# A two-layer attention and expert kernel: softmax work by slices of two duos, and one head's scaling moved to VectorE

## The reference

```python
h = rmsnorm(x, ln_mix[i])
qkv = h @ w_qkv[i]
q = rmsnorm(qkv[..., :nq].reshape(B, S, N_HEADS, HEAD_DIM), q_norm[i])
k = rmsnorm(qkv[..., nq:nq + nk].reshape(B, S, N_KV_HEADS, HEAD_DIM), k_norm[i])
v = qkv[..., nq + nk:].reshape(B, S, N_KV_HEADS, HEAD_DIM)
if i % N_MIXERS == 0:
    q = apply_axial_rope(q, row_cs, col_cs)
    k = apply_axial_rope(k, row_cs, col_cs)
    o = global_attention(q, k, v)          # softmax(q k^T * SCALE) v
else:
    o = window_attention(q, k, v, rel_bias, sinks[i // N_MIXERS])   # with a bias, a window and a sink
x = x + o @ w_o[i]
x = x + hier_moe(rmsnorm(x, ln_ffn[i]), w_group[i], w_expert[i], w1[i], w3[i], w2[i])
```

## Time and profile before

| | us |
|---|---|
| median of 3 runs | 674.86 |
| lowest and highest | 673.85, 676.22 |
| the profiled execution, its own time | 675.01 |
| its span, first to last instruction | 673.2 |
| TensorE busy | 639.0 |
| VectorE, ScalarE, GpSimd busy | 202.7, 177.0, 71.1 |

### The profile page before, as it was taken

One profiled execution on the slowest core, in us unless ns is written; L12 is line 12 of the kernel. 1 busy time (PEld: TensorE's weight loads), 2 busy tenths in 40 slices (PEclk: granted clock), 3 DMA queues, 4 the chain that ended last, 5 costly groups with the idle time before them and its releaser, 6 DMA issues.

```text
span 673.2 us, 7941 instructions
## 1 busy us (share of the span) xinstructions
PE 639.0 (95%) x2947; PEld 283.6 (42%) x2947; DVE 202.7 (30%) x614; ACT 177.0 (26%) x425; POOL 71.1 (11%) x85
## 2 busy tenths in 40 slices
PE   8999899899999999999999887998999999999996
PEld 5444445633433433432354444455344344334332
DVE  1655433512302302301243655234113113113112
ACT  2126642302212112112131554321212112112112
POOL 0006550000000000000010576200000000000000
PEclk9999999899999999999999999997999999999998
DMA  8999706579997999999999993484999799999993
GB/s 323 277 295 422 274 1 272 227 312 421 422 423 294 424 421 423 421 422 421 403 295 249 411 406 79 147 364 153 423 421 422 318 401 421 422 423 423 422 423 125
DMA packets 42882, 229.61 MB, mean 341 GB/s; under 512 B 8207, under 2 KB 8497, under 8 KB 18274
## 3 DMA queue, kind: packets, MB, share of 16 engines
q1 hardware_dynamic: 41212, 224.66, 85.0%
q0 software_dynamic: 1312, 4.23, 2.0%
q10 hardware_dynamic: 326, 0.31, 0.2%
HBM read 228.10 MB, written 1.08 MB: 340 GB/s over the span
## 4 chain that ended last, share of the span: by engine, by line
PE 79%; DMA 9%; DVE 5%; POOL 2%; ACT 2%; issue 1%; SPq 0%; DVEq 0%; POOLq 0%; ACTq 0%
PE ps L1304 28%; PE ps L1331 15%; PE ps L1086 11%; DMA attw<-in_w_dram 8%; PE ps L1168 6%; PE ps L1271 5%; PE ps L1283 4%; POOL attw L413 2%; PE ps L1121 2%; PE ps L1150 2%; PE ps L1137 1%; PE ps L1235 1%; DVE attw L799 1%; PE ps L1313 1%; DMA ring<-in_ln_mix_dram 1%
## 5 line engine op out<-in xcount | busy, mean ns | idle before, releaser
L1304 PE MATMUL ps<-attw,work 128*64 128x512 f32 x512 | 111.7, 592 | 1.5 <-DMA attw<-in_w_dram 1.5
L1304 PE MATMUL ps<-ring,work 128*64 128x512 f32 x512 | 111.4, 593 | 0.0
L1086 PE MATMUL ps<-attw,work 128*128 128x512 f32 x192 | 88.2, 603 | 0.3 <-DVE work L695 0.3
L1331 PE MATMUL ps<-ring,work 128*64 128x512 f32 x384 | 85.7, 595 | 1.1
L931 DVE COPY work<-ps 32x512 f32<-32x512 f32 x64 | 43.7, 683 | 106.1 <-PE ps L1331 105.7
L923 DVE TENSOR_TENSOR work<-work,ps 128x512 f32<-128x512 f32 x16 | 11.0, 688 | 190.3 <-PE ps L1304 190.3
L1304 PEld LDWEIGHTS ps<-attw,work 128*64 128x64 f32 x512 | 36.7, 137 | 75.1 <-issue 71.6
L1304 PEld LDWEIGHTS ps<-ring,work 128*64 128x64 f32 x512 | 36.5, 137 | 72.4 <-issue 72.3
L601 ACT COPY work<-ps 32x512 f32<-32x512 f32 x64 | 36.9, 576 | 107.3 <-PE ps L1331 106.9
L413 POOL TENSOR_SCALAR attw<-attw,stat 128x256 f32<-128x256 f32 x64 | 58.8, 932 | 50.2 <-DVE stat L814 50.0
L1168 PE MATMUL ps<-attw,work 128*128 128x512 f32 x128 | 59.7, 601 | 0.7 <-issue 0.5
(11 more groups left out here) (149 smaller groups left out, 486.4 us busy)
## 6 DMA issues: line engine op xcount, KB each, us to landing
ring<-in_w_dram SPq DMA_DIRECT2D x112, 1024.0 KB, 17.9
attw<-in_w_dram SPq DMA_DIRECT2D x80, 1024.0 KB, 17.5
attw<-in_w_qkv_dram SPq DMA_DIRECT2D x4, 2048.0 KB, 21.0
attw<-in_w_o_dram SPq DMA_DIRECT2D x8, 1024.0 KB, 22.6
attw<-in_w_qkv_dram SPq DMA_DIRECT2D x4, 1024.0 KB, 15.5
ring<-bias_rows POOLq DMA_DIRECT2D x16, 256.0 KB, 6.9
x_sb<-in_x_dram SPq DMA_DIRECT2D x2, 512.0 KB, 6.3
out_dram<-x_sb SPq DMA_DIRECT2D x2, 512.0 KB, 3.6
```

The lines of the kernel that those rows point to most:

```text
L1086: last = pe.matmul(ps[:, g, :], xT[:, k, P * tt:P * tt + P], wqkv[part][:, k, :], start=(k == 0), stop=(k == KB - 1))
L1304: last = pe.matmul(ps[64 * e:64 * e + 64, 6 + which, :], xg[:, k, c:c + 2 * SLOTS], w13(which, k // 4)[:, e, k % 4, :], start=(k == 0), st ...
L1331: last = pe.matmul(ps[64 * e:64 * e + 64, half, :], hT[:, k, 64 * e:64 * e + 64], w2(kh)[:, e, k % 2, 512 * half:512 * half + 512], start= ...
```

## The change

1. `scale_probs` on GpSimd scales head 0 of a duo only. VectorE scales head 1 in `invert_sum`, directly behind the reciprocal (it waits for its own reciprocal's count), and counts a new semaphore `p1_ready`. `turn_probs` turns head 1's two blocks first, behind `p1_ready`, and then waits for `p_ready` and turns head 0's.
2. VectorE's loop goes by slices: both maxima of a slice, then both inversions. The pieces of `head_norm(4)` stand: 0 and 1 at the end of slice 1, 2 between the maxima and the inversions of slice 2, 3 at the end of slice 2; those of `head_norm(5)` the same in slices 3 and 4. `copy_o` stands between the two inversions of slices 3, 5 and 7.
3. `turn_q(2)` and `turn_q(3)` stand ahead of the turning of duo 5 and duo 9; ScalarE's `copy_q(2)` and `copy_q(3)` between `exps` and `copy_probs` of u = 7 and 11; and `square_heads` with `inverse_head_rms` of groups 4 and 5 together behind `copy_probs(1)` and `copy_probs(5)`.

```diff
@@ scale_probs, GpSimd
                 pool.wait_ge(rc_ready, DUOS * L + u + 1)
-                for h in range(2):
-                    last = pool.tensor_scalar(prob[:, u % 4, h, :], prob[:, u % 4, h, :], rc[:, u % 4, h:h + 1], None, ALU.mult)
-                last.then_inc(p_ready, 1)
+                pool.tensor_scalar(prob[:, u % 4, 0, :], prob[:, u % 4, 0, :], rc[:, u % 4, 0:1], None, ALU.mult).then_inc(p_ready, 1)
@@ ScalarE's loop
                 exps(1)
-                square_heads(4)
                 exps(2)
                 copy_probs(0)
                 for u in range(3, DUOS):
                     exps(u)
-                    if u == 3:
-                        inverse_head_rms(4)
-                    if u == 7:
-                        square_heads(5)
-                    if u == 9:
-                        inverse_head_rms(5)
+                    if u in (7, 11):
+                        copy_q((u + 1) // 4)
                     copy_probs(u - 2)
-                    if u == 5:
-                        copy_q(2)
-                    if u == 11:
-                        copy_q(3)
+                    if u in (3, 7):
+                        square_heads(3 + (u + 1) // 4)
+                        inverse_head_rms(3 + (u + 1) // 4)
@@ invert_sum, VectorE
                 dve.reciprocal(rc[:, u % 4, :], total).then_inc(rc_ready, 1)
+                dve.wait_ge(rc_ready, DUOS * L + u + 1)
+                dve.tensor_scalar(prob[:, u % 4, 1, :], prob[:, u % 4, 1, :], rc[:, u % 4, 1:2], None, ALU.mult).then_inc(p1_ready, 1)
@@ VectorE's loop
-                duo_max(L, 0)
-                for u in range(1, DUOS):
-                    duo_max(L, u)
-                    invert_sum(L, u - 1)
-                    if 2 <= u < 6:
-                        head_norm(L, 4, u - 2)
-                    if 8 <= u < 12:
-                        head_norm(L, 5, u - 8)
-                    if u % 4 == 3 and u >= 7:
-                        copy_o(L, u // 4 - 1)
-                invert_sum(L, DUOS - 1)
+                for v in range(SLICES):
+                    g = 4 + v // 3
+                    duo_max(L, 2 * v)
+                    duo_max(L, 2 * v + 1)
+                    if v in (2, 4):
+                        head_norm(L, g, 2)
+                    invert_sum(L, 2 * v)
+                    if v % 2 == 1 and v >= 3:
+                        copy_o(L, v // 2 - 1)
+                    invert_sum(L, 2 * v + 1)
+                    if v in (1, 3):
+                        head_norm(L, g, 0)
+                        head_norm(L, g, 1)
+                    if v in (2, 4):
+                        head_norm(L, g, 3)
@@ turn_probs, TensorE
-                    pe.wait_ge(p_ready, DUOS * L + u + 1)
+                    pe.wait_ge(p1_ready, DUOS * L + u + 1)
...
-                    for t in range(TT):
-                        for h in range(2):
+                    for h in (1, 0):
+                        if h == 0:
+                            pe.wait_ge(p_ready, DUOS * L + u + 1)
+                        for t in range(TT):
@@ TensorE's loop
+                    if v in (2, 4):
+                        turn_q(1 + v // 2)
                     turn_probs(2 * v + 1)
-                    if v == 1:
-                        turn_q(2)
-                    if v == 4:
-                        turn_q(3)
```

More of the change, by code:

```diff
@@ L211, in encoder @@
         qkn_ready, turned, turn_copied = sem("qkn_ready"), sem("turned"), sem("turn_copied")
-        scored, max_ready, exp_done, rc_ready, p_ready = sem("scored"), sem("max_ready"), sem("exp_done"), sem("rc_ready"), sem("p_ready")
+        scored, max_ready, exp_done, rc_ready = sem("scored"), sem("max_ready"), sem("exp_done"), sem("rc_ready")
+        p_ready, p1_ready = sem("p_ready"), sem("p1_ready")
         pt_done, pt_copied, pv_done, o_copied = sem("pt_done"), sem("pt_copied"), sem("pv_done"), sem("o_copied")
```

## The result

| | before | changed |
|---|---|---|
| median, us | 674.36 (4 runs) | 685.36 (4 runs) |
| lowest and highest | 673.75, 676.22 | 683.11, 685.95 |
| ratio, 95% interval | | 1.0165 (1.014 to 1.0191) |
| the profiled execution, its span | 675.01, 673.2 | 685.91, 683.9 |
| TensorE, VectorE, GpSimd busy | 639.0, 202.7, 71.1 | 642.0, 215.0, 46.5 |

The account below looks back on a forecast made before the run. TensorE was taken as the bound, so only its pauses count. 675.0 + 4.2 (layer 0) + 1.0 (layer 1) + 2.4 (clock) = 682.6, less 0.15 for the median: 682.5 us; range 677.0 to 688.5.

Parts of the forecast that it names:

- Direction and mechanism: Attention: turnings 3 and 7 wait through ScalarE's copy and exponentials for maxima behind norm pieces; slower, chance 0.83.
- Turning 3 of layer 0: Turning of duo 3's probabilities: 6.3 us behind turning 1, starting at 63.5 instead of 61.82, +1.7 us.
- Turning 7: Layer 0, turning of duo 7's probabilities: 6.2 us behind the first output copy instead of 3.5, +2.7 us.
- The sum of the two stages: Attention without the clock: +4.2 us in layer 0 and +1.0 us in layer 1.
- The clock: TensorE's clock falls behind two of the four new attention pauses, 1.2 us each: +2.4 us.
- rival 2: TensorE's clock falls behind all four new pauses, at up to 1.8 us each: 687.4 us; chance 0.07.
- VectorE's scaling: VectorE's new 128x256 scaling behind the reciprocal takes 0.25 us, between bounds of 0.17 and 0.47.
- Rival 3: VectorE blocked by GpSimd's scaling for a whole 0.92 us each time: +8 us, 688.5 us; chance 0.08.
- Rival 4: Attention: head_norm's pieces no obstacle, only waits for GpSimd count; 7.2 us go, 667.8 us; chance 0.08.
- Passing the shift on one to one: Any shift of attention's end reaches the kernel's end in full, as expert loads start at points TensorE's progress releases.

Follow-up runs that it names:

- a3: Changed kernel with piece 1 of the norms of query groups 4 and 5 moved behind the next slice's two maxima: 675.78 us.
- b2: Changed kernel with ScalarE's copy of turned probabilities ahead of the next exponentials and two query copies one duo earlier; VectorE's order kept: 669.28 us.
- b1_awake_short: Changed kernel with 10 unused filling matmuls on TensorE ahead of turnings 3 and 7 of both layers: 684.21 us.
- c1_after_again: The changed kernel itself, unedited, timed again: 685.19 us.
- a2: Changed kernel with the split scaling taken back, so GpSimd scales both heads and the new order stays: 684.48 us.
- a1: Kernel before with the split scaling alone, VectorE scaling head 1 and GpSimd head 0, old order kept: 674.33 us.
- b3_split_copy_first: Kernel before with the split scaling and ScalarE's copy of turned probabilities ahead of the next exponentials: 668.87 us.
- b4: Changed kernel's split scaling kept, VectorE's and ScalarE's orders rearranged: most copies ahead of exponentials two duos on, norm pieces spread between maxima: 662.60 us.
- c3: Kernel before with only ScalarE's copy of turned probabilities put ahead of the next exponentials; GpSimd scales both heads: 676.15 us.
- a4: Changed kernel with 20 unused filling matmuls on TensorE ahead of turnings 3 and 7 of both layers: 685.37 us.
- c2: Changed kernel with 10 filling matmuls ahead of turnings 3 and 7 of both layers, timed again: 684.50 us.

## Why the prediction was right, point by point

**Direction and mechanism: right.** The pauses were laid out at 3.2 and 3.7 us in layer 0 and 3.6 and 4.3 in layer 1, and measured 2.90, 3.43, 3.26 and 3.98, each 0.3 shorter. Turning 3 of layer 0 was to start 6.3 us behind the end of turning 1 and starts 6.27 behind it. Turning 7 was to start 6.2 us behind the first output copy and starts 6.17 behind it, at 77.69. The copy in VectorE's timeline:

```profile
71.52 0.69 DVE L816 COPY work<-ps 128x512 f32<-128x512 f32 x1 [5.05 <-PE ps L1151]
```

a3 and b2 cut the path at two of its links and the pauses go.

**The sum of the two stages: right.** Laid out +4.2 and +1.0 us without the clock. b1_awake_short, whose attention shows no fall, has 62.1 and 63.5 us where the kernel before has 58.0 and 62.6: +4.1 and +0.9. The parts agree too, so no large errors cancel: up to turning 7 the terms laid out are +4.7 and +3.5, and b1_awake_short has +4.4 and +3.3; behind it they are -0.5 and -2.5, and it has -0.4 and -2.4.

**The clock: the term that was too small.** I took two falls of 1.2 us, 2.4 in all. The profile shows three, in c1_after_again the same three, at 2.7, 1.6 and 1.6 us, and 5.1 net in the stage. I had subtracted from the price of a fall (1.8 us, from the gathering) a part that would pass while TensorE still waited. Little did: the clock was up for most of the pause and down in the dense work behind it. Windows of layer 0 show it, the first holds the pause before 77.69:

```profile
74.00:78.00 4.00, 0.57 (x3) 0.34 (x3) 3.56 (x12) 2.15 (x9) 0.59 (x1) 0.88 1.04 347
78.00:82.00 4.00, 4.00 (x18) 2.33 (x18) 2.32 (x9) 1.43 (x6) 1.57 (x2) 0.50 0.13 14
82.00:86.00 4.00, 4.00 (x18) 2.34 (x15) 1.06 (x4) 2.71 (x9) 1.08 (x1) 0.76 0.00 0
```

The mean of 0.88 in the first window stands for 0.96 us at the lower level, 0.5; 0.31 of it lies behind 77.69, so about 0.65 us of the pause passed at that level, and over 5 us of dense work behind it. The number of falls was short as well: two were taken, on the ground that none came behind 1.88 us.

5.2 + 5.1 = 10.3 us stands against 10.1 of attention and 11.0 by median. So the truth lay between the forecast and rival 2, and the forecast missed by 2.9 us, nearly all of it in this term. The Trainium skill (TensorE: Matmul & The Clock Gate, part 1) has the clock taken back by idleness; the trace agrees for the pauses of 3.43, 3.26 and 3.98 us, and shows no fall behind that of 2.90, though other runs show falls behind 1.93 to 2.12 us.

**VectorE's scaling: 0.35 us, not 0.25**, inside the bounds of 0.17 and 0.47. The two engines do delay each other, and GpSimd is the one that pays (line views of the changed kernel, ns min/median/max):

```profile
L809 DVE TENSOR_SCALAR attw<-attw,stat x32: 352/353/401, 48.4 to 433.3; 128x256 f32<-128x256 f32 x32
...
L413 POOL TENSOR_SCALAR attw<-attw,stat x32: 933/1081/1087, 48.5 to 433.4; 128x256 f32<-128x256 f32 x32
```

GpSimd's takes 1.08 where it took 0.92, since VectorE starts first, straight behind its own reciprocal; in a2, where VectorE scales nothing, GpSimd's mean is 0.92 again. The Trainium skill (SBUF — State Buffer, section on the two separate sides) gives the shared pair to whichever of the two starts first, for the whole instruction. The trace agrees on who loses, but not on how much: at 54.93 GpSimd starts 0.05 us behind VectorE's 54.88, VectorE goes on for 0.30 more, and GpSimd's scaling is only 0.16 longer. Rival 3, in which VectorE loses 0.92 each time, is refuted; and a1 prices the whole split at 0 (ratio 0.9958 to 1.0013).

**Rival 4, the faster one,** fails where it was to be decided: the bank is not free at turnings 3 and 7. But the 7.2 us that rival 4 saw in the waits for GpSimd were not there to be had even in the old order: a1 took those waits away and gained nothing. With the copy early as well, the split did give 6 us (b3_split_copy_first). The prediction said "if nothing else moved" and let it stand at that; the next wait in line, ScalarE's copy, should have been priced too.

**Passing the shift on one to one: right here, within about 1 us.** From the start of the first products (L1303) to the start of the last scattering (L1282) the experts' stage of layer 0 takes 201.3 us before and after, that of layer 1 200.8 and 202.1; over all fourteen profiled executions that of layer 1 lies between 200.5 and 202.4. The attention's 10.1 us and the median's 11.0 agree that closely partly by luck, since other parts of an execution vary by 1 to 2 us (see the end). In b4, with attention 15.0 us shorter, the two stages take 202.1 and 202.3, and the median is 12.5 us lower, not 15.0; what kept the 2.5 us was not tested.

## What to carry to other kernels

- Where three engines pass a tile around by hand-written queues, write down for one buffer everything that stands ahead of its release on each engine. Here one PSUM bank was freed by a copy behind exponentials behind a maximum behind a rotation, and no single view says so.
- A view of waits names the last of several. Before one is bought off, ask which is next and how much earlier it is: two edits that give 0 and a loss of 0.3% alone gave 1% together.
- A pause of TensorE costs its own length and, where the clock falls, the slow work behind it: price both, and shorten the pause rather than fill it.

## What the runs showed of the hardware

- A scaling of 128x256 float32 values in SBUF takes VectorE 0.353 us and GpSimd 0.92; where VectorE's starts within 0.1 us ahead of GpSimd's, GpSimd's takes 1.08.
- The clock fell behind all nine pauses of 3.02 to 3.98 us that three profiles show (the changed kernel, c1, a2), and behind none of their three of 2.90. The length of a pause alone doesn't decide: it fell behind 1.93 us (a1) and 2.11 (c3), not behind 1.88 (before) or 2.51 (a3); behind pauses of 2.04 to 2.13 us at turning 11 of layer 1 it fell in three profiles (a2, a4, c2) and not in four (the changed kernel, c1, a3, b1). One fall cost 1.6 to 2.9 us of dense work.
- Execution times carry two things that no edit here touches: the first scores of layer 0 start anywhere from 41.9 to 46.4 us, by when the first loads land, and from the start of the last scattering matmuls (L1282) to the end it takes 8.0 to 8.3 us in seven of the fourteen profiled executions and 9.5 to 9.6 in the other seven; the changed kernel has 9.5 in one and 8.2 in another. Between the two kernels of this case they came to -1.9 and +1.5 us. For a change in one stage the length of that stage is the sharper measure, the spans are not.
